# The last expert's second weights by column halves, and the scatter of x ahead of that of ctx

## The chip, the core and the metric

The kernel runs on one core of a Trainium2 chip. The core has a matmul engine (TensorE, PE in the profile, with its weight loads as PEld), VectorE (DVE), ScalarE (ACT), GpSimd (POOL) and SyncE (SP), which issues nearly all transfers from HBM, and 16 DMA engines. The metric is the device time of one execution in microseconds, as the median of several runs; one further execution is recorded by the profiler.

## What is computed

A first block (a state space mixer, one layer) and a second block of two layers, both in float32, on 256 tokens of x and 256 of ctx, 1024 wide. The change touches the end of the expert layer, the norm behind it and the last norm:

```python
def expert_choice_ffn(h, w_router, w1, w3, w2):
    aff = jax.nn.softmax((h @ w_router).astype(jnp.float32), axis=-1)
    gate, idx = lax.top_k(jnp.swapaxes(aff, 1, 2), cap)
    xe = h[bidx, idx]
    hid = jax.nn.silu(jnp.einsum('becd,edf->becf', xe, w1)) * jnp.einsum('becd,edf->becf', xe, w3)
    ye = jnp.einsum('becf,efd->becd', hid, w2) * gate[..., None].astype(h.dtype)
    return jnp.zeros_like(h).at[bidx, idx].add(ye)

# second_block, layer l of 2; ctx (xc) only where need_ctx, in layer 0
h = rms_norm(x, norm_mix[l]) * (1.0 + sc1) + sh1
x = x + g1 * y
h2 = rms_norm(x, norm_ffn[l]) * (1.0 + sc2) + sh2
x = x + g2 * expert_choice_ffn(h2, moe_router[l], moe_w1[l], moe_w3[l], moe_w2[l])
...
return rms_norm(x, final_norm)
```

There are 16 experts with 32 slots each for x and, in layer 0, another 32 for ctx; D and the width of an expert are both 1024.

## The kernel before

**Storage and order.** `mem` is the whole on-chip memory, `bank` one of eight accumulator banks of 128 x 512 floats. Each engine has a program of its own, written out by hand in its order. On TensorE, `B.open` takes the next bank (and waits until its last content was read), `B.close` counts it done; another engine waits with `arrive(name)` for that tile and releases the bank with `took(name)`; `wait_took` waits for that. So what an engine does next is fixed, and a wait holds up all that is written behind it.

**Residual rows.** `xres[:, j, :]` holds 128 tokens by 1024 features; j = 0, 1 are x, j = 2, 3 are ctx (layer 0 only). `xn` holds normed rows, `hT` the same by feature.

**Weights.** Each expert has six pieces of 2 MB (128 partitions x 4096 floats), two each for w1, w3 and w2. SyncE (`load_experts`, issue at L2622) sends the 96 pieces of a layer into 8 slots (layer 0) or 9 (layer 1), each as soon as the piece that was there has been used. Pieces are cut by rows of the matrix: piece 4 has the first 512 rows of w2, piece 5 the last.

**One expert.** Tokens are gathered and transposed (`gather`, `gather_T`), `up` gives the two hidden products, ScalarE and VectorE make `hid` (L1966), transposes give `hidT`, and `down` (the second weights) makes one tile y: first four steps of the contraction with piece 4, then four with piece 5. In layer 0 two column groups of 512 (`n_grp` = 2, `W` = 512) stand in 64 rows of the array each, in layer 1 four of 256 in 32 rows each; they run side by side. VectorE multiplies the four quarters of the tile by the gates into `y_rows` (L1983). Nearly all matmuls share L617 and all transposes L627.

**Scatter.** After every fourth expert, `scatter` spreads four experts' rows over the tokens, eight tiles of 128 x 512 in layer 0 and four in layer 1, and VectorE adds them to `xres` (`sums`, L1948). For the last four experts nothing else runs beside it.

**After layer 0.** ScalarE squares each row tile when its last addition is done (`squares`, L2159), VectorE takes the mean (`mean_squares`, L1445), GpSimd the root of all four (`norm_roots`, L2511), VectorE scales rows 0 and 1 (`norm_rows`, L1493) and ScalarE rows 2 and 3 (`other_rows`, L2165). TensorE, which ran `warm(4)` (four idle matmuls at L624) in the meantime, makes 32 transposes in eight tiles (`norm_T(4)`), and VectorE (L1445) and ScalarE (L2172) modulate them into `hT`. Then come the latent projections lat0 to lat3 with the weights `odd_cq` (VectorE copies and squares them, L1999 to L2003), `krope` and the rest of the odd layer. GpSimd sends the tables of that layer (L2575) when the last addition is done, ahead of the root.

**After layer 1.** The same with two row tiles, `squares(6)`, `mean_squares(6)` and one root; then VectorE scales each row tile with the final gain (L2125) and SyncE stores it (L2639).

## Time and profile before

| | us |
|---|---|
| median of 3 runs | 1952.88 (1951.56 to 1960.87) |
| profiled execution | 1946.83 |
| span of its profile | 1944.9 |

| engine | busy us | share of the span |
|---|---|---|
| TensorE matmul (PE) | 1680.2 | 86% |
| TensorE weight load (PEld) | 859.0 | 44% |
| VectorE (DVE) | 608.9 | 31% |
| ScalarE (ACT) | 348.8 | 18% |
| GpSimd (POOL) | 56.2 | 3% |

The page gives the chain of work that ended last as 56% TensorE, 25% issue (time in which the engine waited for nothing that the profile shows) and 13% transfers.
### The profile page before, as it was taken

The numbers are of one execution on the slowest core, as the hardware profiler recorded it, in microseconds if no ns is written. First come the engines' busy times: TensorE is split into PE (matmuls) and PEld (weight loads), VectorE is DVE, ScalarE is ACT, GpSimd is POOL, SyncE is SP. The second block draws the span as 40 slices with busy tenths as digits, with TensorE's granted clock in tenths as the row PEclk, the third lists the DMA queues.
The fourth block names the chain that finished last, engine by engine and source line by source line (L and its number), as shares of the span: only waits on it lengthen the run. The fifth ranks groups of instructions, "written<-read, shape, count | busy, mean of one in ns | idle before, by whom it ended". The sixth has DMA issues, their size and how long they took to land.

```text
span 1944.9 us, 23321 instructions
## 1 busy us (share of the span) xinstructions
PE 1680.2 (86%) x9754; PEld 859.0 (44%) x9754; DVE 608.9 (31%) x1398; ACT 348.8 (18%) x852; POOL 56.2 (3%) x53
## 2 busy tenths in 40 slices
PE   6999998899999989899999889799998665665664
PEld 3744774446444674333333223265564332232332
DVE  1267839613100872322313222230533110110101
ACT  2222136312011661100000000020431000000000
POOL 1000200100010000000000000000000000000000
PEclk9999999999999999999999999999999888888878
DMA  8512239954132003699999999910327999999996
GB/s 366 213 48 87 95 150 423 424 226 192 55 121 86 1 1 130 246 428 427 428 428 427 429 427 427 423 75 27 130 118 329 426 427 427 427 427 428 426 427 268
DMA packets 39100, 538.17 MB, mean 277 GB/s; under 512 B 4330, under 2 KB 4586, under 8 KB 6612
## 3 DMA queue, kind: packets, MB, share of 16 engines
q1 hardware_dynamic: 37860, 530.80, 65.4%
q0 software_dynamic: 1136, 5.88, 0.8%
q8 instruction: 78, 1.28, 0.3%
q14 instruction: 26, 0.21, 0.0%
HBM read 535.61 MB, written 1.05 MB: 276 GB/s over the span
## 4 chain that ended last, share of the span: by engine, by line
PE 56%; issue 25%; DMA 13%; DVE 4%; ACT 1%; DVEq 1%; POOL 0%; SPq 0%; POOLq 0%; ACTq 0%
PE bank L617 53%; DMA mem<-in_moe 9%; DMA mem<-in_ada_w 2%; PE bank L627 2%; DMA mem<-in_w_ada 1%; DVE mem L1445 1%; DMA mem<-in_w_out 1%; DVEq L1442 1%; ACT mem L2188 0%; PE bank L624 0%; POOL mem L2511 0%; DVE mem L1966 0%; DVE mem L1775 0%; DVE mem L1796 0%; ACT mem L2346 0%
## 5 line engine op out<-in xcount | busy, mean ns | idle before, releaser
L617 PE MATMUL bank<-mem 128*32 128x256 f32 (+10 forms) x8954 | 1573.0, 491 | 240.5 <-DMA mem<-in_moe 164.7
L617 PEld LDWEIGHTS bank<-mem 128*32 128x32 f32 (+3 forms) x8954 | 771.1, 147 | 981.9 <-issue 676.3
L2188 ACT ACTIVATE mem<-bank 128x512 f32<-128x512 f32 (+5 forms) x281 | 139.8, 506 | 1109.1 <-PE bank L617 752.6
L1966 DVE TENSOR_TENSOR mem<-mem,bank 128x512 f32<-128x512 f32 (+1 forms) x32 | 17.8, 557 | 493.9 <-PE bank L617 493.9
L1983 DVE TENSOR_TENSOR mem<-bank,mem 32x512 f32<-32x512 f32 (+1 forms) x128 | 71.1, 555 | 224.9 <-PE bank L617 223.6
L627 PE MATMUL bank<-mem 128*128 128x128 f32 x760 | 120.9, 285 | 15.5 <-DVE mem L1966 5.0
L627 PEld LDWEIGHTS bank<-mem 128*128 128x128 f32 x760 | 88.0, 146 | 82.7 <-issue 46.7
L1599 DVE SCALAR_TENSOR_TENSOR mem<-mem 128x256 f32<-128x256 f32 x160 | 86.9, 543 | 10.4 <-issue 0.9
L1445 DVE TENSOR_SCALAR mem<-bank,mem 128x128 f32<-128x128 f32 (+2 forms) x124 | 40.0, 394 | 40.6 <-PE bank L627 40.5
L2133 ACT ACTIVATE mem<-bank 128x256 f32<-128x256 f32 (+2 forms) x54 | 19.7, 396 | 163.6 <-PE bank L617 163.5
L2511 POOL TENSOR_TENSOR mem<-mem 128x1 f32<-128x1 f32 (+5 forms) x18 | 15.3, 849 | 913.8 <-DVE mem L1445 913.8
L1948 DVE TENSOR_TENSOR mem<-mem,bank 128x512 f32<-128x512 f32 x48 | 32.2, 686 | 7.4 <-PE bank L617 6.9
L1687 DVE TENSOR_TENSOR mem<-bank,mem 128x512 f32<-128x512 f32 x16 | 11.1, 693 | 67.4 <-PE bank L617 67.4
L2269 ACT ACTIVATE mem<-mem 128x128 f32<-128x128 f32 x96 | 30.7, 408 | 0.0
L1750 DVE COPY mem<-bank 128x32 f32<-128x32 f32 x2 | 0.4, 192 | 84.2 <-PE bank L617 84.2
L1445 DVE TENSOR_SCALAR mem<-mem 128x128 f32<-128x128 f32 (+7 forms) x51 | 13.9, 299 | 32.9 <-ACT mem L2193 17.2
L2346 ACT ACTIVATE mem<-bank,mem 128x512 f32<-128x512 f32 (+1 forms) x32 | 18.7, 583 | 19.9 <-DVE mem L1763 19.6
L624 PE MATMUL bank<-mem 128*128 128x512 f32 x40 | 21.7, 694 | 0.0
L1625 DVE TENSOR_TENSOR mem<-mem 128x1536 f32<-128x1536 f32 x12 | 21.0, 1749 | 0.0
L1937 DVE TENSOR_TENSOR mem<-bank,mem 128x256 f32<-128x256 f32 x48 | 18.8, 419 | 5.8 <-PE bank L627 5.7
L1940 DVE TENSOR_TENSOR mem<-mem 128x256 f32<-128x256 f32 x48 | 19.0, 424 | 2.4
L2159 ACT ACTIVATE mem<-mem 128x1024 f32<-128x1024 f32 x10 | 10.6, 1056 | 45.9 <-DVE mem L1948 29.1
(198 smaller groups left out, 522.6 us busy)
## 6 DMA issues: line engine op xcount, KB each, us to landing
mem<-in_moe SPq DMA_DIRECT2D x192, 2048.0 KB, 34.9
mem<-in_ada_w SPq DMA_DIRECT2D x24, 2048.0 KB, 11.5
mem<-in_w_in SPq DMA_DIRECT2D x10, 2048.0 KB, 8.2
mem<-in_w_ada SPq DMA_DIRECT2D x6, 2048.0 KB, 12.2
mem<-in_even_w_in SPq DMA_DIRECT2D x6, 2048.0 KB, 8.0
mem<-in_w_out SPq DMA_DIRECT2D x4, 2048.0 KB, 9.5
mem<-in_odd_w_in SPq DMA_DIRECT2D x3, 2048.0 KB, 19.7
mem<-in_even_w_out SPq DMA_DIRECT2D x2, 2048.0 KB, 7.6
```

What stands on the lines that cost most here:

```text
L617: return nc.tensor.matmul(o, lhsT, rhs, start=start, stop=stop, skip_group_check=True)
L624: nc.tensor.matmul(o, ident, cbuf[:, 0:512], start=True, stop=True, skip_group_check=True)
L627: return nc.tensor.transpose(o, i, ident)
L1442: dve.drain()
L1445: return V.tensor_scalar(o, i, s1, s2, op0, op1)
L1599: last = V.scalar_tensor_tensor(out=xa, in0=src, scalar=w[:, tap:tap + 1], in1=xa, op0=ALU.mult, op1=ALU.add)
L1625: V.tensor_tensor(w, w, cb[:, g, :].unsqueeze(1).to_broadcast([P, 2, 768]), ALU.mult)
L1948: took(f"sc{l}.{b}{j}{h}", V.tensor_tensor(x, x, ps[:, :], ALU.add))
L1983: last = V.tensor_tensor(y_rows[s][r0:r0 + CAP, W * h:W * h + W], ps[CAP * i:CAP * i + CAP, 0:W], gate_ffn[l][CAP * i:CAP * i + CAP, :], A ...
L2133: return S.activation(o, i, ACT.Copy)
L2188: took(name, S.activation(o, i, func))
L2269: last = S.activation(e[:, to:to + P], dec_arg[h % 2][:, P * j:P * j + P], ACT.Exp, bias=col(log_dt, d, q))
```

## The change

1. The host cuts the last expert's w2 by columns: within every column group, the first half of the columns goes to piece 4 (half a), the second to piece 5 (half b), each with all 1024 rows. Piece 5 is sent as two transfers of 1 MB, the first with the rows of the first four steps, counted by `tail_in`.
2. `down_last` makes two tiles, ya and yb, each of eight steps with matmuls half as wide. VectorE multiplies each half by the gates on its own (eight short instructions instead of four), half b's x rows first in layer 0, counted by `y_first`.
3. The last scatter goes x first, then ctx, and in each first the tiles of half a, then of half b. The additions write half of the columns of a row tile in strips.
4. In layer 0, x is normed on its own: mean and root after the first two ctx additions in VectorE's order, one row scaled by VectorE and one by ScalarE, `norm_half(4, 0)`; ctx follows with a root of its own and `norm_half(4, 1)`, which TensorE has between lat1 and lat2. `warm(4)` is no longer run here. GpSimd has the two roots ahead of the tables' transfer.
5. In layer 1, the mean and root of each row tile are apart; the second mean is taken behind the first final scaling.

```diff
                     last.then_inc(half_used, 1)
-                    chunk_freed[f"m{l}.{6 * e + j}"] = (half_used, 3 * EXPERTS * l + 3 * e + j // 2 + 1)
+                    chunk_freed[f"m{l}.{6 * e + j}"] = (half_used, (3 * EXPERTS - 1) * l + 3 * e + j // 2 + 1)
...
                     done_with(f"m{l}.{6 * e + 5}")
+
+                def down_last(e):
+
+                    wait_took(pe, f"ht{l}.{e}")
+                    Wh = W // 2
+                    for half in range(2):
+                        t = B.open(f"y{l}.{e}" + "ab"[half], "dve")
+                        n = f"m{l}.{6 * e + 4 + half}"
+                        if half == 0:
+                            pe.wait_ge(filled[place[n]], 16 * fill_no[n])
+                        else:
+                            pe.wait_ge(tail_in[l], 16)
+                        w = slot(place[n], KT, 512)
+                        for ft in range(8):
+                            if half and ft == 4:
+                                pe.wait_ge(filled[place[n]], 16 * fill_no[n])
+                            for g in range(n_grp):
+                                last = mm(t.ps[S * g:S * g + S, 0:Wh], hT4[:, ft % J, ft // J, :], w[:, ft, Wh * g:Wh * g + Wh], ft == 0, ft == 7)
+                        B.close(t, last)
+                        done_with(n)
+                    for s in range(m["streams"]):
+                        wait_took(pe, f"bs{l}.{EXPERTS // PER - 1}{s}")
+                        for half in range(2):
+                            scatter_half(EXPERTS // PER - 1, half, s)
+
+                def scatter_half(b, half, s):
+
+                    if l == 0 and half and s == 0:
+                        pe.wait_ge(y_first, 1)
+                    else:
+                        wait_took(pe, f"y{l}.{EXPERTS - 1}" + "ab"[half])
+                    for j in range(2 * s, 2 * s + 2):
+                        t = B.open(f"sc{l}.{b}{j}{half}", "dve")
+                        y = y_rows[j // 2].rearrange("p (g h c) -> p g h c", g=n_grp, h=2)[:, :, half, :]
+                        B.close(t, mm(t.ps[:, :], dgT[:, j // 2, P * (j % 2):P * (j % 2) + P], y, True, True))
...
                     B.close(t, last)
-                    down(e)
-                scatter(EXPERTS // PER - 1)
+                    if e < EXPERTS - 1:
+                        down(e)
+                    else:
+                        down_last(e)
 
             route(0)
             experts(0)
 
 
-            norm_T(4)
+            pe.wait_ge(xn_done, NORM_SUM[3] + 2)
+            norm_half(4, 0)
+            wait_took(pe, "nT4a.2")
+            wait_took(pe, "nT4a.3")
             w = use("odd_cq")
             for j in range(4):
+                if j == 2:
+                    pe.wait_ge(xn_done, NORM_SUM[4])
+                    norm_half(4, 1)
+                    wait_took(pe, "nT4b.2")
+                    wait_took(pe, "nT4b.3")
...
 
+            def mean_of(name, j0, j1):
+                dve.wait_ge(sums_done, NORM_SUM[3 if name[4] == "4" else 5] + j1)
+                scaled(meansq[:, j0:j1], ssq[:, j0:j1], 1.0 / D, EPS, ALU.mult, ALU.add).then_inc(ms_done, 1)
+
...
                             took(f"bs{l}.{e // PER}{s}", V.tensor_tensor(dgT[:, s, :], dgT[:, s, :], ps[:, SEQ:2 * SEQ], ALU.mult))
+                    if e == EXPERTS - 1:
+                        break
                     ps = arrive(dve, f"y{l}.{e}")
                     r0 = CAP * (e % PER)
                     for i in range(4):
                         s, h = (i % 2, i // 2) if l == 0 else (0, i)
                         last = V.tensor_tensor(y_rows[s][r0:r0 + CAP, W * h:W * h + W], ps[CAP * i:CAP * i + CAP, 0:W], gate_ffn[l][CAP * i:CAP * i + CAP, :], ALU.mult)
                     took(f"y{l}.{e}", last)
-                sums(EXPERTS // PER - 1)
+                e, Wh = EXPERTS - 1, W // 2
+                r0 = CAP * (e % PER)
+                for half in range(2):
+                    ps = arrive(dve, f"y{l}.{e}" + "ab"[half])
+                    for k, i in enumerate((0, 2, 1, 3)):
+                        s, h = (i % 2, i // 2) if l == 0 else (0, i)
+                        c = W * h + Wh * half
+                        last = V.tensor_tensor(y_rows[s][r0:r0 + CAP, c:c + Wh], ps[CAP * i:CAP * i + CAP, 0:Wh], gate_ffn[l][CAP * i:CAP * i + CAP, Wh * half:Wh * half + Wh], ALU.mult)
+                        if l == 0 and half and k == 1:
+                            last.then_inc(y_first, 1)
+                    took(f"y{l}.{e}" + "ab"[half], last)
+                for s in range(m["streams"]):
+                    for half in range(2):
+                        for j in range(2 * s, 2 * s + 2):
+                            name = f"sc{l}.{EXPERTS // PER - 1}{j}{half}"
+                            ps = arrive(dve, name)
+                            r = xres[:, j, :].rearrange("p (g h c) -> p g h c", g=n_grp, h=2)[:, :, half, :]
+                            took(name, V.tensor_tensor(r, r, ps.rearrange("p (g c) -> p g c", g=n_grp), ALU.add))
+                            if l == 0 and (j, half) == (3, 0):
+                                mean_of("norm4a", 0, 2)
+                                pow_wait("norm4a")
+                                V.tensor_scalar(xn[:, 0, :], xres[:, 0, :], rstd[:, 0:1], None, ALU.mult).then_inc(xn_done, 1)
+                            if l == 1 and (j, half) == (1, 1):
+                                mean_of("norm6.0", 0, 1)
 
             route(0)
             experts(0)
 
 
-            settle()
-            norm_rows(4)
-            norm_T(4)
+            norm_half(4, 0)
+            mean_of("norm4b", 2, 4)
+            pow_wait("norm4b")
+            V.tensor_scalar(xn[:, 2, :], xres[:, 2, :], rstd[:, 2:3], None, ALU.mult).then_inc(xn_done, 1)
             router_scale(1)
             lat_ss, lat_ms = small[:, 64:72], small[:, 80:88]
             for j in range(4):
+                if j == 2:
+                    norm_half(4, 1)
...
             experts(1)
-            settle()
-            mean_squares(6)
             dve.wait_ge(arena_in["gain2"], 16)
             for j in range(2):
+                if j:
+                    mean_of("norm6.1", 1, 2)
+                pow_wait(f"norm6.{j}")
...
 
-            squares(4, sums_of=0)
-            other_rows(4)
-            norm_T(4)
+            def square_of(l, j):
+                wait_took(act, last_sum(l, j))
+                S.activation(xn[:, j, :], xres[:, j, :], ACT.Square, accum_out=ssq[:, j:j + 1]).then_inc(sums_done, 1)
+
+            def other_row(name, j):
+                act.wait_ge(rstd_done, POW.index(name) + 1)
+                S.activation(xn[:, j, :], xres[:, j, :], ACT.Identity, scale=rstd[:, j:j + 1]).then_inc(xn_done, 1)
+
+            for j in range(2):
+                square_of(0, j)
+            other_row("norm4a", 1)
+            norm_half(4, 0)
+            for j in range(2, 4):
+                square_of(0, j)
+            other_row("norm4b", 3)
+            norm_half(4, 1)
...
             experts(1)
-            squares(6, sums_of=1)
+            for j in range(2):
+                square_of(1, j)
...
             load_router(1)
+            for i in range(2):
+                roots("norm4" + "ab"[i], rstd[:, 2 * i:2 * i + 2], meansq[:, 2 * i:2 * i + 2])
             wait_took(pool, last_sum(0, 3))
             pool.dma_start(odd_c, A["odd_tab"]).then_inc(arena_in["odd_tables"], 16)
-            norm_roots(4)
...
             tile_roots(5)
-            norm_roots(6)
+            tile_roots(6)
...
                     e, j = i // 6, i % 6
+                    if i == PIECES - 1:
+
+                        at = SLOT_AT[s]
+                        sp.dma_start(mem[:, at:at + SLOT // 2], A[f"moe{l}"][j, e][:, 0:SLOT // 2]).then_inc(tail_in[l], 16)
+                        sp.dma_start(mem[:, at + SLOT // 2:at + SLOT], A[f"moe{l}"][j, e][:, SLOT // 2:SLOT]).then_inc(filled[s], 16)
+                        last_in_slot[s] = chunk_freed[name]
+                        continue
...
                                  for n in ("moe_w1_2", "moe_w3_2", "moe_w2_2") for half in range(2)])
+
+        by_group = f["moe_w2_2"][l][EXPERTS - 1].reshape(FF, 2 + 2 * l, 2, D // (4 + 4 * l))
+        for half in range(2):
+            o[f"moe{l}"][4 + half, EXPERTS - 1] = col_slabs(by_group[:, :, half, :].reshape(FF, 512), 512)[0]
```

## Rows read from the trace of the kernel before

**Rows 1.** The page: its head.
```profile
span 1944.9 us, 23321 instructions
```

**Rows 2.** Waits of TensorE, 1500 to 1930 us: total us, times, longest us.
```profile
PE bank L617 <- DMA mem<-in_moe: 147.8, 73, 4.1
```

**Rows 3.** Busy time per stretch: length, PE, PEld, DVE, ACT, POOL, clock, DMA, GB/s.
```profile
1600.00:1800.00 200.00, 122.01 (x1464) 58.87 (x1455) 23.41 (x58) 7.73 (x20) 0.00 (x0) 0.83 1.01 427
...
1923.90:1927.60 3.70, 3.59 (x32) 1.81 (x32) 0.00 (x0) 0.00 (x0) 0.00 (x0) 0.54 0.36 155
```

**Rows 4.** Timeline (start, length, idle before), TensorE, last products of layer 0.
```profile
1249.39 3.65 PE L617 MATMUL bank<-mem 128*64 128x512 f32 x16 [0.73 <-ACT mem L2188]
1253.33 3.65 PE L617 MATMUL bank<-mem 128*64 128x512 f32 x16 [0.28 <-DMA mem<-in_moe]
```

**Rows 5.** Timeline, layer 0 behind the products, to the latent projection.
```profile
1257.03 2.81 DVE L1983 TENSOR_TENSOR mem<-bank,mem 32x512 f32<-32x512 f32 x4 [9.08 <-PE bank L617]
...
1260.09 7.12 PE L617 MATMUL bank<-mem 128*128 128x512 f32 x16 [3.11 <-DVE mem L1983]
...
1261.23 0.69 DVE L1948 TENSOR_TENSOR mem<-mem,bank 128x512 f32<-128x512 f32 x1 [1.39 <-PE bank L617]
...
1267.24 0.69 DVE L1948 TENSOR_TENSOR mem<-mem,bank 128x512 f32<-128x512 f32 x1 [0.17 <-PE bank L617]
...
1268.02 1.06 ACT L2159 ACTIVATE mem<-mem 128x1024 f32<-128x1024 f32 x1 [0.56 <-DVE mem L1948]
...
1268.98 0.18 ACT L2159 ACTIVATION_READ_ACCUMULATOR mem<-mem 128x1 f32 x1
...
1269.46 1.04 POOL L2511 TENSOR_TENSOR mem<-mem 128x4 f32<-128x4 f32 x1 [0.66 <-DVE mem L1445]
...
1270.53 2.19 ACT L2165 ACTIVATE mem<-mem 128x1024 f32<-128x1024 f32 x2 [1.37 <-POOL mem L2511]
1270.53 1.42 DVE L1493 TENSOR_SCALAR mem<-mem 128x1024 f32<-128x1024 f32 x2 [1.16 <-POOL mem L2511]
...
1272.78 3.71 PE L627 MATMUL bank<-mem 128*128 128x128 f32 x32 [2.14 <-ACT mem L2165]
...
1273.90 3.76 ACT L2172 ACTIVATE mem<-bank,mem 128x256 f32<-128x256 f32 x8 [1.18 <-PE bank L627]
...
1277.76 52.76 PE L617 MATMUL bank<-mem 128*128 128x384 f32 x217 [1.27 <-DVE mem L1445]
```

**Rows 6.** Timeline, VectorE, lat1 of the latent projection.
```profile
1288.36 0.56 DVE L1999 COPY mem<-bank 128x384 f32<-128x384 f32 x1 [3.82 <-PE bank L617]
...
1289.61 0.08 DVE L2003 DVE_READ_ACCUMULATOR2_ANT mem<- 128x1 f32 x1
```

**Rows 7.** Timeline, layer 1 from the last products to the end.
```profile
1923.98 3.59 PE L617 MATMUL bank<-mem 128*32 128x256 f32 x32 [2.33 <-DMA mem<-in_moe]
...
1928.76 1.93 PE L617 MATMUL bank<-mem 128*32 128x256 f32 x32 [1.19 <-DMA mem<-in_moe]
1930.76 1.74 DVE L1983 TENSOR_TENSOR mem<-bank,mem 32x256 f32<-32x256 f32 x4 [9.61 <-PE bank L617]
...
1932.60 3.68 PE L617 MATMUL bank<-mem 128*128 128x512 f32 x8 [1.91 <-DVE mem L1983]
...
1937.04 1.06 ACT L2159 ACTIVATE mem<-mem 128x1024 f32<-128x1024 f32 x1 [0.57 <-DVE mem L1948]
...
1938.47 0.70 POOL L2511 TENSOR_TENSOR mem<-mem 128x2 f32<-128x2 f32 x1 [461.31 <-DVE mem L1445]
1939.20 2.48 DVE L2125 SCALAR_TENSOR_TENSOR mem<-mem 128x1024 f32<-128x1024 f32 x2 [0.81 <-POOL mem L2511]
```

**Rows 8.** Timeline, TensorE, router products of layer 1 (128 columns).
```profile
1473.87 0.64 PE L617 MATMUL bank<-mem 128*32 128x128 f32 x16
```

**Rows 9.** DMA issues, 1300 to 1400 us: count, KB each, us to landing.
```profile
mem<-in_mla_w_uq SPq DMA_DIRECT2D x1, 768.0 KB, 4.1
mem<-in_mla_w_ukv SPq DMA_DIRECT2D x1, 512.0 KB, 3.3
```

6 lines of the change are left out of this document (4 added, 2 removed).

## The prediction, made before the changed kernel ran

> **What bounds the kernel now.** I read the page first (a span of 1944.9 us [rows 1]), then who TensorE waits for during the experts, then the timeline of the two stretches that the change touches: the end of each layer's experts. In the second layer's experts the core moves 427 GB/s through a 200 us stretch at a granted clock of 0.83, and between 1500 and 1930 us TensorE waits 73 times, 147.8 us in all, for `in_moe` [rows 2, 3]. So this loop runs at the pace of its weights, and work inside it is free as long as the weights arrive; the first layer's last products also stop for their piece, if only by 0.28 us [rows 4]. What is not covered by a transfer is the tail behind the last piece: products, gate multiplication on VectorE, scatter, additions, squares, root, norm, and only then the next large work. Here engines take turns. In layer 0 the last half of products starts at 1253.33 and the latent projection at 1277.76, a tail of 24.43 us [rows 4, 5]. In layer 1 the last half starts at 1928.76 and the two final scalings end at 1939.20 + 2.48 = 1941.68, a tail of 12.92 us [rows 7]. The change is about these two tails, so its whole worth has to be found there.
>
> **Layer 0, up to the products.** By rows of the weights, each half needed its own piece and both filled one tile. By columns, half a has all it needs when the fifth piece is there, and half b runs in two quarters. The number of columns streamed is the same; matmuls double and narrow from 512 to 256 columns. A half took 3.65 us [rows 4], and I keep that: half a 1249.39 to 1253.04, half b right behind, to about 1256.8 (I take 1256.9, against 1256.98 before). The last piece was there by 1253.33, so TensorE, not the landing, ends this: finer waiting gives nothing in layer 0. What it does give is that half a's four multiplications lie beside half b.
>
> **Layer 0, the x half.** The four 32x512 multiplications took 2.81 us [rows 5]. In layer 1 four of 32x256 took 1.74 us [rows 7], 0.435 each; half b has four of these, so y is complete at 1256.97 + 1.74 = 1258.7. The scatter no longer waits for it: products of half a are scattered first. Eight scatter matmuls took 7.12 us from 1260.09 and the first addition began 1.14 us after the first matmul [rows 5]; so from 1256.95 TensorE hands over a tile at 1258.1 and every 0.86 us behind it, the last at 1264.1. The third needs y_first, two multiplications after 1256.97, at 1257.85: no wait. Additions of 0.69 us [rows 5] then end at 1259.5, 1260.1, 1260.75 and 1261.4 for x. ScalarE's square is 1.15 us up to the sum, with the read of the accumulator [rows 5]: 1260.8 to 1261.95, then to 1263.1. VectorE has by then done the first two ctx additions (to 1263.1), and it waits for the sums, takes the mean and waits for GpSimd's root: 0.3 us from the last sum to GpSimd's start [rows 5], and for the root layer 1's row of the same width, 0.70 us [rows 7]: 1264.2. Queued behind these two waits on VectorE are the last two ctx additions, about 1 us late, and behind them only the ctx squares, which ScalarE could not start earlier anyway. Scaling of one row each, 0.7 us on VectorE and 1.1 on ScalarE [rows 5], ends at 1265.3. Sixteen transposes at 3.71/32 us [rows 5] end at 1267.15; ScalarE's eight modulations took 3.76 us [rows 5], so its four end 1.88 us behind their first tile, at 1268.3. The latent projection starts at 1268.35 instead of 1277.76: 9.4 us earlier.
>
> **Layer 0, what is late next.** Part is given back. Before, the latent stage ran uninterrupted: from 1277.76 on, with VectorE's copy of lat1 at 1288.36 [rows 5, 6], so the second pair of products began near 1288.1. Now TensorE ends lat1 at 1278.6, and the ctx rows' squares, root and scaling (ScalarE from 1268.3: 2.3 + 0.3 + 0.7 + 1.1, so 1272.7) are hidden under lat0 and lat1. Not hidden is the ctx half of the transposes: it stands behind lat1 in TensorE's order, 1.86 us to 1280.5, and VectorE reads its tiles only when it has copied and squared lat1, which took from 1288.36 to 1289.7 [rows 6] and so ends about 1280.4, then its four modulations, 1.86 us: 1282.3. The third product starts at 1282.35 against 1288.1. **Layer 0 gives 5.7 us.** The `warm(4)` matmuls that are dropped stood in a wait and cost nothing; what they cover is the clock (below). GpSimd's load of the odd tables moves behind the two roots, to about 1271.7; they are needed by the projection behind `krope`, over 10 us later: nothing. Everything behind is TensorE's own work up to layer 1's experts, whose first loads wait for its tiles; so the weight stream starts 5.7 us earlier and ends 5.7 us earlier.
>
> **Layer 1.** Half a starts where the last half but one did, 1923.98, at the low clock (granted 0.54, so nearly all at 1.2 GHz) and took 3.59 us [rows 3, 7]. Matmuls of 128 columns on 32-wide weights: sixteen records took 0.64 us at the full clock [rows 8], so the 32 records of a quarter take 1.3 us, and 1.8 (half of 3.59) at the low clock. From 1927.6 the third quarter ends at 1928.9 to 1929.4, the last at 1930.2 to 1931.2; before, the products ended at 1930.69. I take 1930.4: 0.3 gained, bounds +0.5 and -0.5. Multiplications of 32x128: from 0.69 and 0.435 for 512 and 256 columns, 0.30 each by the same slope (estimate from the rows), 1.2 us instead of 1.74. Scatter starts at once: tiles at E + 1.17, 2.03, 2.9, 3.75, with E the end of the products; the last addition ends at E + 4.4; before, it released the square at 1937.04 [rows 7], E + 6.35. The squares start at E + 3.6 and end at E + 4.75 and 5.9. The first row's mean and root (0.3 + 0.70) lie beside the second square, its scaling (1.24, half of 2.48) is E + 5.75 to 7.0; only then come the second mean and root, and the second scaling ends at E + 9.2, against E + 10.99. The early first row is worth little, since the second stands behind it. **Layer 1 gives 1.8 + 0.3 = 2.1 us.**
>
> **Rules against the change.** Sixteen 128-column records in 0.64 us are 40 ns each [rows 8]. The Trainium skill (TensorE: Matmul & The Clock Gate, Back-to-back issue gap) gives about 81 ns for each pair of weight load and 128-column matmul; by it a quarter would take 2.6 us and layer 1 gain 0.8 us instead of 2.1. The row of this kernel's own form contradicts it, and decides. And small transfers here: 0.5 MB took 3.3 us and 0.75 MB 4.1 [rows 9], so 1.7 us are fixed and each MB takes 3.2. Beside this row: the skill (DMA: Bandwidth & Descriptors, Bandwidth) puts a transfer of 1 MB at 78% of the peak.
>
> **The sum.** 5.7 + 2.1 = 7.8 us. The profiled execution took 1946.83 us with a span of 1944.9; it would take 1939.0. The median of before, 1952.88, lies 6.05 above that execution; I forecast the median, 1952.88 - 7.8 = **1945.1**. Half a per cent, about what a measurement of this kernel can tell from no change, is 9.8 us: the forecast lies inside it, on the side of faster.
>
> **Rivals.** (1) *Both tails at their good ends*, chance 0.19. Layer 0 at 7.0 (ctx modulations beginning beside lat1's squares, worth up to 1.3) and layer 1 at 3.0 give 10: 1942.9 or below, faster by over 0.5%. The wide idle spaces of ScalarE there speak for it, VectorE's written order against it. (2) *The split transfer lands late*, 0.10: if the fixed 1.7 us is paid by the second part and not hidden under the first, layer 0 keeps its sum (TensorE reaches the last quarter at 1255 for a landing at 1253.33) and layer 1 loses 1.7: 1946.8. Against it: the whole stream shows no such gap at 427 GB/s. (3) *The clock falls in layer 0's new tail*, 0.06, the one that ends slower. The granted clock averaged 0.83 over a stretch in which TensorE was busy 122 of 200 us [rows 3], so it falls in this kernel where gaps repeat, and the `warm(4)` matmuls are gone. At half clock the eight scatters cost 6.9 us more, sixteen transposes 1.9, lat0 5.1: 13.9 - 7.8, so 1959.0; it decides from about 8 us of added TensorE time. Against it: the new stretch from 1257 to 1282 has idle spaces of only 1.3, 1.2 and 1.9 us, where before TensorE idled 3.11 us ahead of the scatter [rows 5] and the scatter still ran at 0.86 us a tile. (4) *The gain is lost behind layer 0*, by a wait that is not TensorE's, the tables or a weight load, 0.05: layer 1's part alone, 1950.8.
>
> **Chances.** The forecast itself, 1943.2 to 1947.5, has 0.60. The range 1940 to 1951 takes in rivals 1, 2 and 4 and the bounds of the products and leaves out 3 and more than the bounds say. Faster by over 0.5%: 0.21 (rival 1 and a little scatter of the medians). Slower by over 0.5%: 0.03, rival 3 with the low clock kept further into the stage; the rest of rival 3 is a loss inside the bound. Within: 0.76.
>
> **What would show it.** Right: lat0 starts 14 to 16 us behind the landing of the last piece instead of 24; an idle space of about 1.9 us before the third latent product, put down to VectorE; the stream of layer 1 unchanged in length; the last scaling 9 to 10 us behind the last product; granted clock 1.00 through layer 0's tail. Wrong: a product half clearly over 3.65 us in layer 0, strided additions of more than 0.69 us, an idle space before the last quarter larger than the 1.19 us of before [rows 7], or a granted clock below 1.00 in the scatter.

## The result, and the profile after

| | before | after |
|---|---|---|
| median of the runs shown | 1955.18 us (4 runs, 1951.56 to 1960.87) | 1937.62 us (4 runs, 1936.95 to 1938.05) |
| profiled execution | 1946.83 us | 1938.05 us |
| span of it | 1944.9 us [rows 1] | 1935.8 us |

The ratio is 0.9913 (0.9897 to 0.9929), some 17 us. The forecast was 1945.1 with a range from 1940 to 1951: the direction was right, the time lies below the range, and "within 0.5%" was wrong. Yet the two profiled executions differ by 8.8 us, one more than the sum of 7.8. Of the 28 further executions of before that stand beside the first four kernels below, one (2641.78 us, at a granted clock of 0.625) was disturbed and is left out of the ratios. So there are two questions: were the parts of the sum right, and why do the medians lie twice as far apart as the profiles?

In all that follows, a tail is counted from "half a", the start of the first half of the last expert's products.

The head of the page after, with the busy row and the granted clock in 40 slices:

```profile
span 1935.8 us, 23514 instructions
...
PE 1678.1 (87%) x9842; PEld 863.3 (45%) x9842; DVE 610.3 (32%) x1408; ACT 347.6 (18%) x852; POOL 57.3 (3%) x55
...
PEclk9999999999999999999999999999999887887878
```

Of the 193 instructions more, 176 are TensorE's: 96 matmul records more in the narrower products, 8 fewer since `warm(4)` is gone, and as many weight loads. The timeline of after, layer 0 behind the products, answers to [rows 4] to [rows 6]. Columns: start, length, engine, line, operation, then in brackets the idle time ahead of it and what ended that.

```profile
1253.04 14.21 PE L619 MATMUL bank<-mem 128*64 128x256 f32 x80 [0.69 <-ACT mem L2268]
1256.76 1.74 DVE L2045 TENSOR_TENSOR mem<-bank,mem 32x256 f32<-32x256 f32 x4 [5.12 <-PE bank L619]
1260.21 1.76 DVE L2045 TENSOR_TENSOR mem<-bank,mem 32x256 f32<-32x256 f32 x4 [1.71 <-PE bank L619]
1262.00 2.53 DVE L2055 TENSOR_TENSOR mem<-mem,bank 128x512 f32<-128x512 f32 x4
1263.92 1.06 ACT L2521 ACTIVATE mem<-mem 128x1024 f32<-128x1024 f32 x1 [10.94 <-DVE mem L2055]
...
1266.42 0.72 POOL L2605 TENSOR_TENSOR mem<-mem 128x2 f32<-128x2 f32 x1 [465.80 <-DVE mem L1492]
1267.18 1.15 ACT L2525 ACTIVATE mem<-mem 128x1024 f32<-128x1024 f32 x1 [1.07 <-POOL mem L2605]
...
1268.38 1.97 PE L629 MATMUL bank<-mem 128*128 128x128 f32 x16 [1.13 <-ACT mem L2525]
...
1271.54 10.56 PE L619 MATMUL bank<-mem 128*128 128x384 f32 x32 [1.19 <-DVE mem L1492]
...
1281.93 1.91 PE L629 MATMUL bank<-mem 128*128 128x128 f32 x16
...
1283.55 1.90 DVE L1492 TENSOR_SCALAR mem<-bank,mem 128x256 f32<-128x256 f32 x4
1285.50 15.77 PE L619 MATMUL bank<-mem 128*128 128x128 f32 x86 [1.66 <-DVE mem L1492]
```

What is to be seen here:

- The first line holds products and scatter in one run of 80 records without a gap: the 3.11 us ahead of the scatter [rows 5] are gone.
- The latent projection starts 18.50 us behind half a; before, 1277.76 - 1249.39 = 28.37 [rows 4, 5]. That is 9.87 earlier.
- Its third product starts 32.46 us behind half a, behind an idle space of 1.66 us put down to VectorE. Before it began near 1288.1 (estimated from VectorE's copy of lat1 at 1288.36 [rows 6]), 38.7 behind half a. Layer 0's tail gives 6.2 us.

The same view of layer 1, against [rows 7]:

```profile
1917.97 4.10 PE L619 MATMUL bank<-mem 128*32 128x128 f32 x96 [0.87 <-DMA mem<-in_moe]
1921.25 1.21 DVE L2045 TENSOR_TENSOR mem<-bank,mem 32x128 f32<-32x128 f32 x4 [4.90 <-PE bank L619]
1922.79 4.73 PE L619 MATMUL bank<-mem 128*32 128x128 f32 x40 [0.73 <-DMA mem<-in_moe]
...
1923.94 1.20 DVE L2045 TENSOR_TENSOR mem<-bank,mem 32x128 f32<-32x128 f32 x4 [1.49 <-PE bank L619]
...
1929.47 1.28 DVE L2205 SCALAR_TENSOR_TENSOR mem<-mem 128x1024 f32<-128x1024 f32 x1 [0.72 <-POOL mem L2605]
...
1930.90 0.54 POOL L2605 TENSOR_TENSOR mem<-mem 128x1 f32<-128x1 f32 x1 [1.53 <-DVE mem L1492]
1931.48 1.28 DVE L2205 SCALAR_TENSOR_TENSOR mem<-mem 128x1024 f32<-128x1024 f32 x1 [0.66 <-POOL mem L2605]
```

From half a to the last landing (the start of the last quarter of products) there are 4.82 us; before, 1928.76 - 1923.98 = 4.78. From that landing to the end of the span there are 13.0 us; before, 1944.9 - 1928.76 = 16.1. Layer 1's tail gives 3.1 us. Together 9.3 us, and the spans differ by 9.1.

Last, the granted clock per stretch in after (length; PE, PEld, DVE, ACT and POOL busy; clock; DMA share; GB/s):

```profile
1260.00:1267.00 7.00, 7.00 (x18) 2.93 (x16) 5.68 (x11) 2.19 (x4) 0.58 (x1) 1.00 0.98 419
1267.00:1272.00 5.00, 2.67 (x19) 2.09 (x19) 3.79 (x7) 3.64 (x6) 0.14 (x1) 1.00 0.28 121
1272.00:1282.00 10.00, 10.00 (x33) 5.84 (x32) 2.80 (x9) 2.66 (x5) 2.55 (x3) 1.00 0.32 111
```

**What the two profiles agree on by accident.** They are alike outside the tails only in sum. Layer 0's experts begin at 813.21 in before and at 816.82 in after, with the same code ahead of them: 3.6 us against after. Behind layer 0, a run of 62 records that follows an idle space of 1.93 us goes the other way. In before, then in after:

```profile
1365.03 23.20 PE L617 MATMUL bank<-mem 128*64 128x512 f32 x62 [1.93 <-issue]
```

```profile
1362.48 20.17 PE L619 MATMUL bank<-mem 128*64 128x512 f32 x62 [1.93 <-issue]
```

The same records, the same idle space, 3.0 us of difference: in before TensorE's granted clock was 0.50 from 1365 to 1371 us, in after 1.00. This row led to the theory below. In the prediction I had taken the idle spaces ahead of the scatter at the lengths, and at the clock, of one execution.

### The profile page after: what moved, and what is told of

Read it like the earlier page. It is cut to its first block, busy times and chain, and to the rows that moved or that the text cites. A ratio compares the mean times of both kernels' runs of the same rounds, so it can differ in the third digit from the quotient of the medians.

```text
span 1935.8 us, 23514 instructions
## 1 busy us (share of the span) xinstructions
PE 1678.1 (87%) x9842; PEld 863.3 (45%) x9842; DVE 610.3 (32%) x1408; ACT 347.6 (18%) x852; POOL 57.3 (3%) x55
## 4 chain that ended last, share of the span: by engine, by line
PE 61%; DMA 32%; DVE 4%; issue 1%; ACT 1%; DVEq 1%; POOL 0%; SPq 0%; POOLq 0%; ACTq 0%
PE bank L619 57%; DMA mem<-in_moe 27%; PE bank L629 3%; DMA mem<-in_ada_w 3%; DMA mem<-in_w_ada 1%; DVE mem L1492 1%; PE bank L626 1%; DVEq L1489 1%; DMA mem<-in_w_out 1%; ACT mem L2268 0%; DVE mem L2017 0%; POOL mem L2605 0%; DVE mem L1826 0%; DVE mem L1847 0%; ACT mem L2426 0%
## 5 line engine op out<-in xcount | busy, mean ns | idle before, releaser
L619 PEld LDWEIGHTS bank<-mem 128*32 128x32 f32 (+2 forms) x9050 | 776.0, 147 | 969.1 <-issue 674.8
L2036 DVE TENSOR_TENSOR mem<-bank,mem 32x512 f32<-32x512 f32 (+1 forms) x120 | 66.6, 555 | 209.1 <-PE bank L619 207.9
L1999 DVE TENSOR_TENSOR mem<-mem,bank 128x512 f32<-128x512 f32 x36 | 23.9, 685 | 3.7 <-PE bank L619 3.4
L2339 ACT ACTIVATE mem<-bank 128x512 f32<-128x512 f32 x24 | 14.3, 595 | 23.3 <-DVE mem L1492 17.9
```

The costliest lines, as they stand in the source:

```text
L619: return nc.tensor.matmul(o, lhsT, rhs, start=start, stop=stop, skip_group_check=True)
L1999: took(f"sc{l}.{b}{j}{h}", V.tensor_tensor(x, x, ps[:, :], ALU.add))
L2036: last = V.tensor_tensor(y_rows[s][r0:r0 + CAP, W * h:W * h + W], ps[CAP * i:CAP * i + CAP, 0:W], gate_ffn[l][CAP * i:CAP * i + CAP, :], A ...
```

## The experiments

**Theory A:** in the kernel before, TensorE's clock falls in most executions in its idle spaces ahead of the last scatters (3.11 us in layer 0, 1.91 in layer 1), and the profiled execution was one in which it didn't. The change removes both spaces, and so saves the fallen clock besides the 9.3 us. Before the first runs below I put this saving at 8 to 9 us. **The rivals:** the durations are all, and the rest of the 17 us is chance in a few runs of before; or the changed layers give more than their tails show.

### The kernel before, once more

No edit.

> The kernel before, unchanged, once more. Theory A (TensorE's clock falls in the idle space ahead of the scatter in some executions of the kernel before, and in none of the changed one): its executions spread over 8 us or more, from about 1947 to 1961, and a profile of one of the longer executions has a granted clock below 1.00 in layer 0's tail (some 1257 to 1280 us) or layer 1's (1930 to 1937). Rival B (the spread comes from elsewhere, such as the weight stream or the stages before the experts): the same spread, but granted clock 1.00 in both tails and the tails as long as in the first profile, 24.4 us from the last product half to the latent projection and 16.1 us from the last product half to the end.

Measured: 1953.66 us (12 runs, 1948.5 to 1960.46), beside 1953.67 for 28 more of the same kernel; ratio 0.9998 (0.9983 to 1.0014). The profiled execution of before, 1946.83, lies below all 40 (of 24 more that ran beside later kernels one is lower, 1945.1). The new profile (execution 1951.65) shows the timeline of TensorE in both tails, and one stretch of the clock:

```profile
1256.68 3.65 PE L617 MATMUL bank<-mem 128*64 128x512 f32 x16 [0.29 <-DMA mem<-in_moe]
1263.44 8.81 PE L617 MATMUL bank<-mem 128*128 128x512 f32 x16 [3.11 <-DVE mem L1983]
...
1277.82 5.38 PE L627 MATMUL bank<-mem 128*128 128x128 f32 x32 [2.13 <-ACT mem L2165]
1284.39 11.78 PE L617 MATMUL bank<-mem 128*128 128x384 f32 x43 [1.20 <-DVE mem L1445]
```

```profile
1935.73 5.37 PE L617 MATMUL bank<-mem 128*128 128x512 f32 x8 [1.91 <-DVE mem L1983]
```

```profile
1263.00:1270.00 7.00, 6.56 (x12) 2.84 (x13) 3.23 (x6) 1.58 (x3) 0.00 (x0) 0.76 0.58 246
```

The idle space is the same 3.11 us, but the 16 scatter records take 8.81 us instead of 7.12 and the 32 transposes 5.38 instead of 3.71 [rows 5], at a granted clock of 0.76 around the scatter. From the last half to the latent projection there are 27.71 us instead of 24.43: 3.3 us. In layer 1 the scatter takes 5.37 us instead of 3.68 [rows 7]: 1.7 more. So what the change takes away is worth up to 5.0 us more in such an execution than in the one I read.

Two things are to be kept apart here. The clock was still 1.00 through both idle spaces and fell only behind them, some 1.0 us into each scatter (near 1264.4 and 1936.7 us). And the transposes lost their 1.7 us in a fall of their own: the clock was back at 1.00 from 1269 to 1277.8, through the warm matmuls, and fell behind the next idle space, of 2.13 us. The tails are not all that differs, either. Half a of layer 0 starts at 1252.73 here and at 1249.39 in the first profile, 3.3 us later, while the 62 records of above took 20.17 us, 3.0 less; these two nearly cancel.

### Layer 0 alone, layer 1 alone

Both kernels are the changed one with one layer set back. For layer 0 alone:

```diff
-                    if e < EXPERTS - 1:
+                    if l == 1 or e < EXPERTS - 1:
...
-                    if i == PIECES - 1:
+                    if l == 0 and i == PIECES - 1:
...
-            tile_roots(6)
+            norm_roots(6)
```

and for layer 1 alone:

```diff
-                    if e < EXPERTS - 1:
+                    if l == 0 or e < EXPERTS - 1:
...
-            norm_half(4, 0)
-            mean_of("norm4b", 2, 4)
-            pow_wait("norm4b")
...
+            settle()
+            norm_rows(4)
+            norm_T(4)
```

> The change in layer 0 alone; layer 1 as before. By the sum of the prediction it gives 5.7 us (about 6.2 by the landmarks of the changed profile) and layer 1 the rest. Theory A: the part that the sum lacks, about 9 us, belongs mostly to the layer whose tail loses its clock; if that is layer 0, this kernel is 12 to 16 us faster than before (ratio about 0.993) and its executions lie close together. Rival B: 6 us faster (ratio 0.997), with the spread of before.

> The change in layer 1 alone; layer 0 as before. By the sum of the prediction it gives 2.1 us (about 3 by the landmarks). Theory A with layer 0 as the place: 2 to 3 us faster (ratio 0.9985) and the spread of before stays. If layer 1's tail is the place: 10 us or more faster (ratio 0.995 or less) and no spread.

Measured: layer 0 alone 1945.4 us, ratio 0.995 (0.9933 to 0.9967), 8.3 us below before by the medians; layer 1 alone 1949.1 us, ratio 0.9973 (0.996 to 0.9985), 4.6 below. Each gives more than its tail in the profiles, 6.2 and 3.1, by 2.1 and 1.5 us; layer 0 alone lies between what theory A (12 to 16) and rival B (6) gave for it. The surplus is thus smaller than I had put it, and is not one layer's. Each profile also holds the tail that was left as it was. Layer 1's scatter in the kernel with layer 0 alone, then layer 0's in the kernel with layer 1 alone (timelines of TensorE):

```profile
1926.30 2.78 PE L619 MATMUL bank<-mem 128*32 128x256 f32 x32 [2.83 <-DMA mem<-in_moe]
1930.98 5.20 PE L619 MATMUL bank<-mem 128*128 128x512 f32 x8 [1.89 <-DVE mem L2044]
```

```profile
1266.82 8.58 PE L619 MATMUL bank<-mem 128*128 128x512 f32 x16 [3.11 <-DVE mem L2030]
```

Both scatters ran at the fallen clock for a part. But the fall in layer 1 came ahead of the idle space of 1.89 us: the last half of products took 2.78 us, not the 1.93 of the half in front of it, and the granted clock is 0.50 from 1927.5 us on, through the idle space and into the scatter. It followed the 2.83 us for which TensorE waited for the last piece. In layer 0's tail it came in the last 0.5 us of the 3.11 (0.50 from 1266.5 on). So the scatter behind the space of 3.11 us was slow in two of three profiles and that behind 1.9 us in two of three, in one of these because the clock was low already; and the profile on which I predicted is the one in three for both.

### The kernel before, with the idle spaces filled

Matmuls that compute nothing are put into the two idle spaces of the kernel before, ahead of the wait for y: six records in layer 0, four in layer 1.

```diff
+                    if b == EXPERTS // PER - 1:
+                        warm(3 - l)
```

> The kernel before with idle matmuls of 128 x 512 that fill the wait ahead of the last scatter: three in layer 0 (2.6 us in an idle space of 3.1) and two in layer 1 (1.7 in 1.9). They compute nothing that is used. Theory A: the clock no longer falls there, the long executions go, and the median drops by some 8 us to about 1947 (ratio 0.996) with all executions within 1 or 2 us. Rival B: nothing, 1951 to 1961 as before (ratio 1.000).

Measured: 1949.84 us (12 runs), ratio 0.9978 (0.9966 to 0.999), 3.8 us below before. Timeline of TensorE, both tails:

```profile
1262.75 3.65 PE L617 MATMUL bank<-mem 128*64 128x512 f32 x16 [0.31 <-DMA mem<-in_moe]
1266.34 2.84 PE L624 MATMUL bank<-mem 128*128 128x512 f32 x6
1269.31 7.14 PE L617 MATMUL bank<-mem 128*128 128x512 f32 x16
```

```profile
1935.43 2.84 PE L617 MATMUL bank<-mem 128*32 128x256 f32 x32 [2.85 <-DMA mem<-in_moe]
1938.20 2.72 PE L624 MATMUL bank<-mem 128*128 128x512 f32 x4
1940.76 3.60 PE L617 MATMUL bank<-mem 128*128 128x512 f32 x8
```

Hardly a step comes earlier by this edit. In layer 0 the scatter starts 6.56 us behind the last half of products instead of 6.76 [rows 4, 5]. In layer 1 the clock had again fallen within the last products (2.84 us, and 0.50 from 1936.5 us on), behind a wait of 2.85 us for their piece. The unused matmuls ran at it and the clock was back at 1.00 by 1940, so that the scatter took 3.60 us; it starts 2.56 us behind the last product instead of 1.91. What the edit gains, but for those 0.2 us, is clock.

This is the run that shows a fallen clock in the median, and it shows less than I expected: 3.8 us with an interval from 2.0 to 6.6, not some 8, and executions spread over 6.6 us (1948.29 to 1954.91), not 1 or 2. The profiled one is the slowest of the twelve although its layer 0 tail ran at full clock; half a of layer 0 started at 1258.79 in it, 9.4 us later than in the first profile, ahead of all that was edited. With 6.2 and 3.1 us of durations the 3.8 make 13.1. The profiles agree roughly: against the first one, the three with layer 0's space lost 0, 3.3 and 1.5 us in its tail and the three with layer 1's 0, 1.7 and 2.4, on average 1.6 and 1.3 (an estimate from six values).

### The changed kernel, once more

No edit; it ran twice, on two other chips, each time beside more runs of before.

> The changed kernel, unchanged, once more. The two layers alone gave 8.3 and 4.6 us against the same runs of before, 12.9 in all. Theory A (work saved as summed, 6 and 3 us, and besides a fallen clock avoided in each layer's tail): the two add up, so 12 to 15 us faster than before (ratio 0.992 to 0.994), and the profile has a granted clock of 1.00 from the products through the scatter in both tails. Rival C (the two layers' edits help each other, as the first 17 us suggest): 16 us or more (0.992 or below) with a place in the profile that neither layer alone explains.

> The changed kernel once more, as the partner of the three others on this chip. From the two measurements so far (17 and 14 us faster than before) and the two layers' 12.9 in sum: 13 to 16 us faster, ratio 0.992 to 0.993.

Measured: 1939.1 us against 1954.45, ratio 0.9927 (0.9908 to 0.9946); and 1939.95 against 1952.74, ratio 0.9933 (0.9912 to 0.9954). By the ratios 14.3 and 13.1 us: what the account gives, within its uncertainty. The 17 us of the first comparison are at the upper end, with only four runs on each side: its 1937.62 lies 1.5 and 2.3 below the two later medians of this kernel, its 1955.18 lies 0.7 to 2.4 above the three later ones of before. Its interval overlaps both.

### The scatter waits for y again

The order of the changed kernel stays, but TensorE waits for the gate multiplications of half b before its first scatter. This gives back an idle space.

```diff
                     for s in range(m["streams"]):
                         wait_took(pe, f"bs{l}.{EXPERTS // PER - 1}{s}")
+                    wait_took(pe, f"y{l}.{e}b")
```

> The changed kernel, but TensorE waits for all of half b's multiplications before it scatters anything, in both layers: an idle space of about 1.8 us in layer 0 and 1.3 in layer 1 is back, everything else as changed. By durations alone it costs 1.8 us in layer 0 and 1.2 in layer 1, 3.0 in all. Theory A: besides this the clock falls in some executions, which makes the scatter take up to 1.7 us longer in each layer and spreads the executions: 4 to 6 us slower than the changed kernel. Rival (the clock has no part in it, or needs the longer idle space of 3.11 us): 3.0 us slower and the scatter at 0.86 us a tile.

Measured: 1943.91 us, ratio 0.9951 (0.9933 to 0.9969), 4.8 us above the changed kernel measured beside it. Timeline of TensorE, both tails:

```profile
1255.13 7.13 PE L619 MATMUL bank<-mem 128*64 128x256 f32 x64 [0.69 <-ACT mem L2269]
1264.12 7.15 PE L619 MATMUL bank<-mem 128*128 128x512 f32 x16 [1.86 <-DVE mem L2046]
...
1289.53 6.96 PE L619 MATMUL bank<-mem 128*128 128x128 f32 x39 [1.66 <-DVE mem L1493]
```

```profile
1929.42 3.72 PE L619 MATMUL bank<-mem 128*128 128x512 f32 x8 [1.33 <-DVE mem L2046]
```

The idle spaces of 1.86 and 1.33 us cost their own length: the third latent product starts 34.40 us behind half a instead of 32.46. The clock did not fall in this profile. The surplus over some 3.3 us fits theory A by its size, but the profile doesn't show it, and 1.5 us are within the uncertainty of two medians of six runs. This run doesn't decide; it shows only that starting the scatter with half a is worth these spaces.

### Layer 0's norm joint again

Products and scatter stay as changed; the norm of layer 0 is one step for all four rows again, with its `warm(4)`.

```diff
-            norm_half(4, 0)
-            mean_of("norm4b", 2, 4)
-            pow_wait("norm4b")
-            V.tensor_scalar(xn[:, 2, :], xres[:, 2, :], rstd[:, 2:3], None, ALU.mult).then_inc(xn_done, 1)
+            settle()
+            norm_rows(4)
+            norm_T(4)
```

> The changed kernel, but layer 0's norm is again one for all four row tiles, with the warm matmuls and 32 transposes in one go; column halves, x-first scatter and layer 1 as changed. The last ctx addition then ends some 7.9 us behind the products (before: 10.96), so of layer 0's 6.2 us the halves and the early scatter account for 3.5 and the separate norm of x for 2.7. Expected 2.7 us slower than the changed kernel if the sum of durations holds; near 0 if the ctx half between lat1 and lat2 gives all of it back; 6 if the halves are worth nothing on their own.

Measured: 1944.6 us, ratio 0.9951 (0.9932 to 0.997), 5.5 us above the changed kernel by the medians and 4.7 by the ratios. Timeline of TensorE:

```profile
1254.22 14.20 PE L619 MATMUL bank<-mem 128*64 128x256 f32 x80 [0.69 <-ACT mem L2253]
...
1279.36 16.82 PE L619 MATMUL bank<-mem 128*128 128x384 f32 x70 [1.27 <-DVE mem L1484]
```

The projection starts 25.14 us behind half a and runs through. The first two products take 10.39 us (from 1271.54 to 1281.93 in after), so the third starts 35.5 behind half a: 3.0 us later than in after. So the split norm carries about half of layer 0's 6.2 us, and the order of products and scatter the other half. The 1.7 to 2.5 us above that I cannot assign.

### A longer idle space on the changed kernel

As the kernel with the wait for y, and in layer 0 VectorE also makes two additions whose results nobody reads, before half b's multiplications. The space becomes longer than the 3.11 us of before.

```diff
+                    wait_took(pe, f"y{l}.{e}b")
...
+                    if l == 0 and half:
+                        for _ in range(2):
+                            V.tensor_tensor(xg, silu_h, silu_h, ALU.add)
+                            settle()
```

> The changed kernel, TensorE again waiting for all of half b's multiplications before any scatter, and in layer 0 two additions of 128x512 on VectorE ahead of these multiplications that nothing uses (1.4 to 1.6 us), so that TensorE's idle space there is 3.3 us, about the 3.11 of before, instead of 1.86. By durations it costs 1.9 + 1.5 us in layer 0 and 1.3 in layer 1, 4.7 us against the changed kernel. Theory A (an idle space of this length lets the clock fall in most executions, one of 1.86 rarely): the scatter of layer 0 takes 8.5 us or more instead of 7.15 in the profile, and the kernel is 6.5 to 8 us slower than the changed one, about 1947, with a spread of 5 us or more. Rival: 4.7 us and scatter 7.15.

Measured: 1944.08 us (8 runs), ratio 0.9956 (0.9938 to 0.9974), 4.1 us above the changed kernel measured beside it. Timeline of TensorE:

```profile
1252.35 7.13 PE L619 MATMUL bank<-mem 128*64 128x256 f32 x64 [0.69 <-ACT mem L2273]
1262.88 7.15 PE L619 MATMUL bank<-mem 128*128 128x512 f32 x16 [3.39 <-DVE mem L2050]
...
1288.29 11.88 PE L619 MATMUL bank<-mem 128*128 128x128 f32 x68 [1.66 <-DVE mem L1493]
```

Here theory A, as I had put it, misses. An idle space of 3.39 us, longer than that of before, left the clock whole in the profile, and the medians differ by about what the durations do (35.94 us from half a to the third latent product, 3.5 more than in after, and the space in layer 1). So the length of a space alone doesn't decide. What differs is what TensorE did ahead of it: here 7.13 us of products in one run, in before two runs of 3.65 us with 0.28 us between and 0.73 ahead [rows 4], after a stream with such gaps in both. Whether that is the reason is not settled by these runs. The eight times fall into two groups, 1941.63 to 1942.91 and 1945.25 to 1947.84, and the profiled execution (1942.18) is of the lower: in the upper group the clock may have fallen. No profile shows that, and what runs ahead of the tails differs by more than this between executions.

### Three attempts to get more

The ctx half of layer 0's transposes goes between the first and the second latent product, and in layer 1 the second mean ahead of the first scaling:

```diff
-                if j == 2:
+                if j == 1:
                     pe.wait_ge(xn_done, NORM_SUM[4])
                     norm_half(4, 1)
+                if j == 2:
                     wait_took(pe, "nT4b.2")
...
+            mean_of("norm6.1", 1, 2)
...
-                if j:
-                    mean_of("norm6.1", 1, 2)
```

> The changed kernel with two reorderings: the ctx half of the transposes stands between lat0 and lat1 instead of between lat1 and lat2, so that its modulations lie beside lat1, and in layer 1 the second mean is taken before the first final scaling. By the changed profile, the 1.66 us idle space ahead of the third latent product goes (the ctx rows are scaled 1 us before lat0 ends) and the second scaling ends about 0.4 us earlier: 2.0 us faster than the changed kernel. Rival: TensorE waits for the ctx rows behind lat0 instead, and nothing is gained.

Measured: 1939.72 us, ratio 0.9931 (0.991 to 0.9951), the same as the changed kernel. In its timeline the idle space before the third product is gone: the second product starts at 1280.47, 25.49 us behind half a, and the third by lat0's length 5.23 behind it, so 1.7 us earlier than in after. The profile lost the same again behind it (TensorE), and layer 1 gained nothing (VectorE and GpSimd):

```profile
1280.47 15.88 PE L619 MATMUL bank<-mem 128*128 128x384 f32 x80
...
1362.50 21.87 PE L619 MATMUL bank<-mem 128*64 128x512 f32 x62 [1.92 <-issue]
```

```profile
1931.69 1.27 DVE L2205 SCALAR_TENSOR_TENSOR mem<-mem 128x1024 f32<-128x1024 f32 x1
1931.85 1.52 POOL L2605 TENSOR_TENSOR mem<-mem 128x1 f32<-128x1 f32 x1 [0.57 <-DVE mem L1493]
1933.40 1.29 DVE L2205 SCALAR_TENSOR_TENSOR mem<-mem 128x1024 f32<-128x1024 f32 x1 [0.44 <-POOL mem L2605]
```

The one-column root takes 1.52 us beside VectorE's scaling and 0.54 alone. It starts 0.16 us behind the start of the scaling, ends 0.41 behind its end, and the second scaling starts no sooner (8.70 us behind the last landing, against 8.69 in after). And behind the idle space of 1.92 us at 1360 the clock was low again: in 2 of 12 profiles (before and this one), with 20.17 or 20.18 us in the others. Two more kernels fill that space with four matmuls that compute nothing; the second also has the earlier ctx transposes, with layer 1 as in the changed kernel.

```diff
+            warm(2)
             wait_took(pe, "ckvT")
```

> The changed kernel with two idle matmuls (1.7 us) in the 1.93 us that TensorE waits ahead of the kv projections at 1363 us. After this space the 62 records took 20.17 us in eight of ten profiles and 23.20 and 21.87 in two, where the clock had fallen. Theory A: the profile has 20.17, and on average the fill is worth 0.2 x 2.4, about 0.5 us: not to be told from the changed kernel (ratio between them 1.000). Rival (the fill delays the work behind it): 1 us or more slower.

> The changed kernel with the ctx half of the transposes between lat0 and lat1 and the same fill, layer 1's means as in the changed kernel. The earlier ctx half gave 1.8 us by its landmarks in the profile and lost 1.7 to a fallen clock behind the kv wait. With the fill both should hold: 1.8 to 2.3 us faster than the changed kernel, some 1937 against 1939. If it is the same again, 1.8 us are lost in a place that the profile has yet to show.

Timeline of TensorE in the first of them:

```profile
1361.75 1.88 PE L626 MATMUL bank<-mem 128*128 128x512 f32 x4
1363.80 20.20 PE L619 MATMUL bank<-mem 128*64 128x512 f32 x62 [0.16 <-DVE mem L2113]
```

Measured: 1939.72 us, ratio 0.9931 (0.9909 to 0.9953), for the filling alone, the same as the changed kernel: where the clock falls in 2 of 12 profiles, filling can't be seen in a median. With both, 1937.06 us, ratio 0.9919 (0.9898 to 0.994), 2.9 us below the changed kernel measured beside it (1939.95); the 1.7 us of the shorter tail are contained in that. It is the fastest kernel of the study, though its interval overlaps that of the changed one, and that of the filling alone.

## Why the prediction was right where it was, and wrong where it was

**Layer 0, the x half (right).** The projection was to start at 1268.35 instead of 1277.76, 9.4 us earlier; it came 9.87 earlier against half a. The products were to end at "about 1256.8" with VectorE's multiplications taking 1.74 us; they took 1.74 and 1.76, and the additions 2.53 for four, so strided additions cost no more than before. Both halves of products took 7.13 us (the kernel with the wait for y) where I had 7.5. No duration was off by half a microsecond; small ones added up to the 0.5 us.

**Layer 0, what is late next (right, a size off).** The idle space before the third product was there, put down to VectorE, with 1.66 us instead of 1.9. Layer 0 gave 6.2 us in place of 5.7. Rival 1 wanted 7.0 here, which did not come; its 3.0 in layer 1 did (below), and the sum of 9.3 lies nearer its 10 than the forecast's 7.8. Its mechanism in layer 0, ctx modulations beside lat1's squares, would have needed another order on VectorE, as the kernel with earlier ctx transposes has it.

**Layer 1 (right, sizes off).** The second scaling was to end at E + 9.2. In the third profile of the changed kernel, 32 records of a quarter take 1.08 us; by this E is 1923.9, and the scaling ends at 1932.76, E + 8.9. The products gained 0.8 us and not 0.3: the last quarter ran at the full clock where I allowed for the low one, and took 1.08 us where I had 1.3 at that clock. Here that quarter is, in the third profile:

```profile
1919.97 1.08 PE L619 MATMUL bank<-mem 128*32 128x128 f32 x32 [0.49 <-DMA mem<-in_moe]
```

Layer 1 gave 3.1 us in place of 2.1. The Trainium skill (TensorE: Matmul & The Clock Gate, Back-to-back issue gap) has some 81 ns for a weight load and matmul of this width; 1.08 us for 32 records are 34 ns each. The trace does not agree, and it decides, as it had to for the forecast.

**The split transfer (rival 2, fell).** From half a to the last quarter there are 4.82 us against 4.78: the second part of the piece lands when the whole had. Waits for `in_moe` between 1500 and 1925 us come to 143.0 us in 70 places, against 147.8 in 73 over a stretch 5 us longer [rows 2]; from layer 1's router products to the last half a there are 449.7 us against 450.1, so the stream kept its length.

```profile
PE bank L619 <- DMA mem<-in_moe: 143.0, 70, 4.3
```

**The clock in the new tail (rival 3, fell the other way round).** I asked whether the clock would fall in the new tail and found it improbable, by the row of 3.11 us at the full clock [rows 5]. The new tail did stay at 1.00. But the same row misled me on the old one: it is one execution, and in the two other profiles that hold this space unchanged the clock fell at its end or behind it. This is **the step that failed**: "1952.88 lies 6.05 above that execution; I forecast the median, 1952.88 - 7.8". It takes the 6.05 us as a constant that the change leaves alone. And the sum of 7.8 prices both old tails at the clock of that one execution: the clock that the change saves in the others stands in it at nothing. The filled spaces alone brought the kernel before from 1953.67 to 1949.84, 3.8 us. How much of the 6.05 us this is, no run shows exactly. A part lies ahead of the change, where the forecast was right to keep it: half a of layer 0 started at 1249.39 in this profile and between 1252.35 and 1258.79 in the thirteen others. Had I asked what a median execution does that the lucky one doesn't, the candidates stood in the rows: two idle spaces of TensorE, of 3.11 and 1.91 us, right in the tails to be changed, in a kernel whose granted clock averaged 0.83 over a stretch with TensorE busy 122 of 200 us [rows 3]. The price was there as well, at half clock "the eight scatters cost 6.9 us more", though the part of it that came was 1.7 in a scatter and 1.7 in the transposes.

**The sum.** 5.7 + 2.1 = 7.8 against 6.2 + 3.1 = 9.3: 1.5 us of the miss. The clock saved in before's spaces, 3.8 measured by itself (2.0 to 6.6): the larger part. Together 13.1 us, beside 14.3 and 13.1 in the two later comparisons and 17 in the first. What more there is in the first is not explained; four runs stood on each side. The two later medians of the changed kernel, 1939.1 and 1939.95, lie just below the range as well, so the miss is not that chance alone. Of the signs that were named, the granted clock of 1.00 and the idle space ahead of the third product came; the last scaling ended 8.9 us behind the last product, just under the 9 to 10.

**Rival 4** (gain lost behind layer 0) fell. The start of layer 1's last products came 6.0 us earlier in the profile, but that this is near 5.7 is luck: after's execution was 3.6 us late at half a of layer 0 and gained 3.0 in the 62 records. Counted from half a it came 9.7 us earlier, the 6.2 of the tail, the 3.0 of clock and 0.4 more.

## What to carry to other kernels

Look where the profiled execution lies among the runs before a sum is made on it. If it is the fastest, its idle spaces on TensorE may be ones at which the clock happened to hold, and a change that closes such a space can save more in the median than in the profile: price it at both clocks. Look also at how far the executions differ ahead of the change, since that part stays. An order that lets TensorE go from one kind of work to the next without a stop (here products of both halves, then scatter) is worth the space and what follows the space. To tell the two apart, fill the space with matmuls that compute nothing: what that gains is clock, as long as nothing starts earlier by it.

## What the runs showed of the hardware that was not expected

- One profile shows one draw of the clock. The same 3.11 us of idle were followed by a scatter of 7.12, 8.81 or 8.58 us; the same 1.9 us by 3.68, 5.37 or 5.20 (in the last the clock was low before the space began); the same 1.93 us elsewhere by 20.17 us ten times, and by 23.20 and 21.87.
- A fall need not come within the idle space: at 1264.4 and 1936.7 us it came some 1.0 us into the scatter behind it, near 1927.2 and 1936.3 within products that followed a wait of 2.8 us. Matmuls that compute nothing let the clock come back ahead of the scatter (3.60 us), where an idle space did not (5.20), in one profile each.
- Length of the space isn't all: 3.39 us behind 7.13 us of unbroken products cost no clock in the one profile taken. Why is open.
- A one-column root on GpSimd took 0.54 us alone and 1.52 us beside VectorE's 1.27 us scaling, ending 0.41 us behind it: a step moved beside VectorE's work may not come earlier at all.
- Halving the last transfer into two pieces in a full queue cost nothing: 4.82 us against 4.78.
